# A fifth seven-product pair in each column pair of the down projection, in a new order of the pairs, with the MLP's squares on ScalarE

## The reference

```
proj = rmsnorm(x, norm1_g[l]) @ w_in[l]          # 2048 x 4352, split among the mixers A, B, C
x = x + concat(A, B, C) @ w_out[l]
h2 = rmsnorm(x, norm2_g[l])
x = x + square(relu(h2 @ w_up[l])) @ w_down[l]   # 2048 x 8192 and 8192 x 2048
```

## Time and profile before

| What | Value |
|---|---|
| Time, median of 3 runs | 2037.56 us (2037.42 to 2037.96) |
| The profiled execution: its own time | 2036.9 us |
| Its span | 2035.1 us |
| TensorE busy | 2028.2 us |
| VectorE busy | 1517.8 us |
| ScalarE busy | 1161.0 us |
| GpSimd busy | 228.0 us |

### The profile page before, as it was taken

One profiled execution on the slowest core, in us unless ns is written; L12 is line 12 of the kernel. 1 busy time (PEld: TensorE's weight loads), 2 busy tenths in 40 slices (PEclk: granted clock), 3 DMA queues, 4 the chain that ended last, 5 costly groups with the idle time before them and its releaser, 6 DMA issues.

```text
span 2035.1 us, 27169 instructions
## 1 busy us (share of the span) xinstructions
PE 2028.2 (100%) x10602; PEld 1702.0 (84%) x10602; DVE 1517.8 (75%) x1953; ACT 1161.0 (57%) x1540; POOL 228.0 (11%) x224
## 2 busy tenths in 40 slices
PE   9999999999999999999999999999999999999999
PEld 8887788888888888888888877888888888888887
DVE  7767566788779769868777775666887796797785
ACT  6557644466456457545545576445654564565463
POOL 6253100000000000002123531000000000000000
PEclk9999999999999999999999999999999999999999
DMA  9477866677668667766664778666776686677664
GB/s 304 131 230 190 219 199 181 185 217 230 187 196 246 197 197 211 224 189 202 199 177 142 219 196 229 187 183 188 228 216 189 196 244 193 202 214 219 189 205 137
DMA packets 182816, 411.36 MB, mean 202 GB/s; under 512 B 14122, under 2 KB 22800, under 8 KB 182688
## 3 DMA queue, kind: packets, MB, share of 16 engines
q1 hardware_dynamic: 173968, 379.52, 60.7%
q0 software_dynamic: 8544, 30.01, 8.1%
q10 hardware_dynamic: 176, 0.09, 0.0%
HBM read 377.95 MB, written 2.12 MB: 187 GB/s over the span
## 4 chain that ended last, share of the span: by engine, by line
PE 99%; DVE 1%; DMA 0%; issue 0%; SPq 0%; ACT 0%; ACTq 0%
PE psum L635 23%; PE psum L611 21%; PE psum L638 12%; PE psum L615 10%; PE psum L678 10%; PE psum L681 5%; PE psum L645 3%; PE psum L649 3%; PE psum L646 3%; PE psum L728 2%; PE psum L729 2%; PE psum L732 2%; PE psum L743 1%; PE psum L817 1%; PE psum L796 0%; PE psum L842 0%
## 5 line engine op out<-in xcount | busy, mean ns | idle before, releaser
L940 ACT CAST w_hi<-raw_ring 128x1024 fp32r<-128x1024 f32 (+1 forms) x720 | 743.7, 1041 | 710.1 <-PE psum L638 322.6
L1180 DVE TENSOR_TENSOR w_lo<-raw_ring,w_hi 128x1024 fp32r<-128x1024 f32 (+1 forms) x664 | 811.4, 1230 | 387.3 <-ACT w_hi L940 385.6
L635 PE MATMUL psum<-xt,w_hi 128*128 128x512 f32 x2048 | 513.3, 392 | 0.3 <-issue 0.3
L635 PEld LDWEIGHTS psum<-xt,w_hi 128*128 128x128 f32 x2048 | 368.8, 189 | 67.0 <-issue 0.7
L638 PEld LDWEIGHTS psum<-xt,w_lo 128*128 128x128 f32 x2048 | 279.4, 190 | 20.0
L638 PE MATMUL psum<-xt,w_lo 128*128 128x256 f32 x2048 | 285.6, 282 | 0.0
L611 PE MATMUL psum<-w_hi,xt 128*128 128x512 f32 (+1 forms) x1152 | 281.5, 386 | 0.1
L611 PEld LDWEIGHTS psum<-w_hi,xt 128*128 128x128 f32 x1152 | 202.4, 188 | 40.8 <-issue 2.9
L1737 POOL DMA_DIRECT2D lo_own<-raw_ring x28 | 24.3, 866 | 1361.2 <-ACT lo_own L956 1361.2
L678 PE MATMUL psum<-w_hi,ht_lo 128*128 128x512 f32 x448 | 174.4, 389 | 0.0
L678 PE MATMUL psum<-w_hi,ht_hi 128*128 128x512 f32 x448 | 174.4, 389 | 0.0
(11 more groups left out here) (212 smaller groups left out, 2462.1 us busy)
## 6 DMA issues: line engine op xcount, KB each, us to landing
raw_ring<-in_w_up_dram SPq DMA_DIRECT2D x256, 512.0 KB, 4.1
raw_ring<-in_w_down_dram SPq DMA_DIRECT2D x256, 512.0 KB, 4.6
raw_ring<-in_w_in_dram SPq DMA_DIRECT2D x128, 512.0 KB, 4.6
raw_ring<-in_w_out_dram SPq DMA_DIRECT2D x64, 512.0 KB, 4.9
w_lo<-raw_ring POOLq DMA_DIRECT2D x28, 512.0 KB, 6.6
lo_own<-raw_ring POOLq DMA_DIRECT2D x28, 512.0 KB, 6.8
raw_ring<-in_w_in_dram SPq DMA_DIRECT2D x16, 256.0 KB, 2.8
x<-in_x_dram SPq DMA_DIRECT2D x8, 256.0 KB, 7.6
```

The costliest lines, as they stand in the source:

```text
L635: pe.matmul(bank[:, f, :], w_hi[:, w, j, f * P:(f + 1) * P], both, start=kt == 0, stop=False, skip_group_check=True)
L940: act.copy(w_hi[:, u % AHEAD, :, 0:cols], raw_ring[:, u % RAWS, :, 0:cols]).then_inc(hi_ready, 1)
L1180: dve.tensor_tensor(w_lo[:, u % AHEAD, :, 0:cols], raw_ring[:, u % RAWS, :, 0:cols], w_hi[:, u % AHEAD, :, 0:cols].bitcast(F32), ALU.subtr ...
```

## The change

- The pairs of a column pair are taken in the order of `ORDER`, `kp` 0, 1, 3, 2, 5, 6, 4, 7, and the places 1, 2, 4, 5 and 7 of it use seven products (`SEVEN_AT`). So `kp = 6` (`EXTRA`) is new among them, and places 1 and 2, and 4 and 5, are neighbours.
- For the second of two neighbours, `t_hi` and `t_lo` are made two units later in the queues of ScalarE and VectorE (`follows_seven`), and its weight sums are begun behind the first one's `t_lo`.
- The token sums of `kp = 6` are made apart: VectorE at step 5 (`sums_of`), ScalarE's `extra_hi` at step 6, VectorE's `extra_lo` at step 7 of `d = 0`. TensorE waits for them (`extra_done`) before place 5. They lie over `head_in`, which is free by then.
- The other token sums move one step later.
- The last chunk: VectorE's two operations L1566 and L1568 become one (relu, times `row_scale`), and ScalarE squares the result twice, once into `ht_hi` and once in place. `row_scale` now holds the root, which GpSimd works out.
- The units with a low part by DMA are `m0` and `m12`, in place of `m0` and `m8`.
- Four transposes of x in the tail of layer 0 (`T_USE`, the x1 panels) come one step later.

```diff
@@ -76,15 +76,19 @@
 KPS = 8
 SEVEN = (1, 3, 5, 7)
 BLOCKS = {b: [kp % 4 for kp in SEVEN if kp // 4 == b] for b in range(2)}
-SEVENS = (LOOPS * 2 + 1) * len(SEVEN)
+EXTRA = 6
+ORDER = [(0, 1, 3, 2, 5, EXTRA, 4, 7)] * 2
+SEVEN_AT = [(1, 2, 4, 5, 7)] * 2
+TURN_SEVENS = sum(len(at) for at in SEVEN_AT)
+SEVENS = LOOPS * TURN_SEVENS + len(SEVEN_AT[0])
 BANK_MOVES = (2 * LOOPS + 1) * 4
...
 SUMMED_UNITS = list(range(55, 83, 2))
-SUMMED_PAIR = [LOOP0 + LOOP_UNITS * i + 16 * d + m for i in range(LOOPS) for d in range(2) for m in (0, 8)]
-SUMMED_PAIR += [DOWN3, DOWN3 + 8]
+SUMMED_PAIR = [LOOP0 + LOOP_UNITS * i + m for i in range(LOOPS) for m in (0, 12, 16, 28)]
+SUMMED_PAIR += [DOWN3, DOWN3 + 12]
...
 for _n in range(4):
-    T_USE[DOWN3 + 21 + 2 * _n] = ("x1", _n)
+    T_USE[DOWN3 + 22 + 2 * _n] = ("x1", _n)
...
+        with ExitStack() as extra:
+            extra_hi, extra_lo = [extra.enter_context(nc.sbuf_tensor(f"extra_{h}", [P, 4, P], F32R)) for h in ("hi", "lo")]
...
+        def follows_seven(pl, u):
+
+            return seven_at(pl, u) is not None and seven_at(pl, u - 2) is not None
...
-                kp, half = m // 2, m % 2
+                kp, half = ORDER[d][m // 2], m % 2
...
-                if kp in SEVEN:
+                if m // 2 in SEVEN_AT[d]:
...
-                i, first, last = SEVEN.index(kp), kp == SEVEN[0], kp == KPS - 1
+                first, last = kp == SEVEN[0], kp == KPS - 1
                 _, number = seven_at(pl, s)
                 if d == 0:
                     pe.wait_ge(s_done, pl.l * 2 * TURNS + 2 * pl.i + kp // 4 + 1)
+                if kp == EXTRA:
+                    pe.wait_ge(extra_done, pl.l * TURNS + pl.i + 1)
                 if first and d == 0:
                     pe.wait_ge(evicted[0], pl.evictions(18))
...
                 def s_tile(n):
-                    return [t[:, i, n, :] for t in (s_hi, s_lo)]
+                    if kp == EXTRA:
+                        return [t[:, n, :] for t in (extra_hi, extra_lo)]
+                    return [t[:, SEVEN.index(kp), n, :] for t in (s_hi, s_lo)]
...
                 act.wait_ge(unit_done, pl.unit(u + 1))
+                if follows_seven(pl, u - 2) and seven_at(pl, u - 2)[0] == 1:
+                    t_hi_of(seven_at(pl, u - 2)[1])
                 seven = seven_at(pl, u)
                 if seven is not None and seven[0] == 0:
                     act.wait_ge(t1_ready, seven[1] + 1)
                 act.copy(w_hi[:, u % AHEAD, :, 0:cols], raw_ring[:, u % RAWS, :, 0:cols]).then_inc(hi_ready, 1)
-                if seven is not None and seven[0] == 1:
-                    act.wait_ge(t_raw_ready, seven[1] + 1)
-                    if seven[1]:
-                        act.wait_ge(sevens_done, seven[1])
-                    act.copy(t_hi[:, :, :], t_raw[:, :, :]).then_inc(t_hi_ready, 1)
+                if seven is not None and seven[0] == 1 and not follows_seven(pl, u):
+                    t_hi_of(seven[1])
                 if is_summed(pl, u) and not has_own_lo(pl, u):
                     act.activation(w_lo[:, u % AHEAD, :, :], raw_ring[:, u % RAWS, :, :], ACT.Copy, scale=-1.0).then_inc(lo_negated, 1)
+
+            def t_hi_of(number):
+
+                act.wait_ge(t_raw_ready, number + 1)
+                if number:
+                    act.wait_ge(sevens_done, number)
+                act.copy(t_hi[:, :, :], t_raw[:, :, :]).then_inc(t_hi_ready, 1)
...
                     act.wait_ge(relu2, pl.at(H_CHUNKS, count + 1, 4))
-                    act.copy(ht[0][:, 4 * q:4 * q + 4, :].rearrange("p k n -> p (k n)"), mlp_t[q % 2][:, :]).then_inc(h_hi, 1)
-                made = sums_made(pl, s, part, c, k, 2)
+                    act.activation(ht[0][:, 4 * q:4 * q + 4, :].rearrange("p k n -> p (k n)"), mlp_t[q % 2][:, :], ACT.Square)
+                    act.activation(mlp_t[q % 2][:, :], mlp_t[q % 2][:, :], ACT.Square).then_inc(h_hi, 1)
+                made = sums_made(pl, s, part, c, k, 3)
                 if made is not None:
                     b, count = made
                     act.wait_ge(s_raw_ready, count + 1)
                     _, where, nb = s_places(b)
                     act.copy(s_hi[:, where, :, :], s_raw[:, 0:nb, :, :]).then_inc(s_hi_ready, 1)
+                if part == "pair" and c == 0 and k == 6:
+                    act.wait_ge(extra_raw, pl.l * TURNS + pl.i + 1)
+                    act.copy(extra_hi[:, :, :], s_raw[:, 0, :, :]).then_inc(extra_cast, 1)
...
+                if follows_seven(pl, u - 2) and seven_at(pl, u - 2)[0] == 1:
+                    t_lo_of(seven_at(pl, u - 2)[1])
+                after, seven = seven_at(pl, u + 1), seven_at(pl, u)
+                if after is not None and after[0] == 0 and seven is None:
                     first_sums(pl, u + 1)
-                seven = seven_at(pl, u)
                 if seven is not None and seven[0] == 0:
                     dve.wait_ge(t2_ready, seven[1] + 1)
                     dve.tensor_tensor(t_raw[:, 2, :], raw_ring[:, (u + 1) % RAWS, 0, :], t_raw[:, 1, :], ALU.subtract).then_inc(t_raw_ready, 1)
                 dve.wait_ge(hi_ready, pl.unit(u + 1))
                 dve.tensor_tensor(w_lo[:, u % AHEAD, :, 0:cols], raw_ring[:, u % RAWS, :, 0:cols],
                                   w_hi[:, u % AHEAD, :, 0:cols].bitcast(F32), ALU.subtract).then_inc(split_done, 1)
+                if seven is not None and seven[0] == 1:
+                    if pair_at(pl, u)[1:] == (1, 2 * SEVEN_AT[1][0] + 1):
+                        take_totals(pl, pair_at(pl, u)[0])
+                    if not follows_seven(pl, u):
+                        t_lo_of(seven[1])
+                    if after is not None:
+                        first_sums(pl, u + 1)
                 if after is not None and after[0] == 0:
                     dve.wait_ge(t1_ready, after[1] + 1)
                     dve.tensor_tensor(t_raw[:, 1, :], raw_ring[:, (u + 2) % RAWS, 1, :], raw_ring[:, (u + 1) % RAWS, 1, :],
                                       ALU.subtract).then_inc(t2_ready, 1)
-                if seven is not None and seven[0] == 1:
-                    if pair_at(pl, u)[1:] == (1, 2 * SEVEN[0] + 1):
-                        take_totals(pl, pair_at(pl, u)[0])
-                    dve.wait_ge(t_hi_ready, seven[1] + 1)
-                    dve.tensor_tensor(t_lo[:, :, :], t_raw[:, :, :], t_hi[:, :, :].bitcast(F32), ALU.subtract).then_inc(t_lo_ready, 1)
+
+            def t_lo_of(number):
+
+                dve.wait_ge(t_hi_ready, number + 1)
+                dve.tensor_tensor(t_lo[:, :, :], t_raw[:, :, :], t_hi[:, :, :].bitcast(F32), ALU.subtract).then_inc(t_lo_ready, 1)
...
-                fs = slice(own.start - 8 * b, own.stop - 8 * b, own.step)
+                sums_of(slice(own.start - 8 * b, own.stop - 8 * b, own.step), nb, s_raw_ready)
+
+            def sums_of(fs, nb, ready):
+
...
                 else:
-                    link(total)
-                    link(dve.tensor_scalar(tot, tot, 1.0 / D, EPS, ALU.mult, ALU.add))
-                    dve.reciprocal(rstd[:, 1, :], tot).then_inc(rstd_ready, 1)
+                    total.then_inc(row_total2, 1)
...
-                    link(dve.scalar_tensor_tensor(mlp_t[q % 2][:, :], mlp_t[q % 2][:, :], 0.0, mlp_t[q % 2][:, :], ALU.max, ALU.mult))
                     v = mlp_t[q % 2][:, :].rearrange("p (f q) -> p f q", f=4)
-                    dve.tensor_tensor(v, v, row_scale[:, :].unsqueeze(1).to_broadcast([P, 4, SEQ]), ALU.mult).then_inc(relu2, 1)
-                made = sums_made(pl, s, part, c, k, 1)
-                if made is not None:
-                    dve.wait_ge(relu2, late_count(pl, s))
-                    token_sums(made[0])
-                made = sums_made(pl, s, part, c, k, 3)
+                    dve.scalar_tensor_tensor(v, v, 0.0, row_scale[:, :].unsqueeze(1).to_broadcast([P, 4, SEQ]), ALU.max, ALU.mult).then_inc(relu2, 1)
+                made = sums_made(pl, s, part, c, k, 4)
...
+                made = sums_made(pl, s, part, c, k, 2)
+                if made is not None:
+                    token_sums(made[0])
+                if part == "pair" and c == 0 and k == 5:
+                    sums_of(slice(EXTRA % 4, EXTRA % 4 + 1), 1, extra_raw)
+                if part == "pair" and c == 0 and k == 7:
+                    dve.wait_ge(extra_cast, pl.l * TURNS + pl.i + 1)
+                    dve.tensor_tensor(extra_lo[:, :, :], s_raw[:, 0, :, :], extra_hi[:, :, :].bitcast(F32), ALU.subtract).then_inc(extra_done, 1)
...
+                    if u == SUMMED_PAIR[0]:
+                        pool.wait_ge(row_total2, pl.l + 1)
+                        rsqrt(rstd[:, 1, :], small[:, 4, 0:RT], RT, 1.0 / D).then_inc(rstd_ready, 1)
```

20 lines of the change are left out of this document (9 added, 11 removed).

## The result

The changed kernel takes 2140.82 us (median of 4 runs, 2139.66 to 2144.63), the kernel before 2037.49 us (4 runs, 2037.15 to 2037.96): a ratio of 1.051, 95% interval 1.0497 to 1.0524. It is 103 us slower. The forecast was 2123 us, in a range of 2085 to 2155. The profiled execution of after took 2139.92 us, its span 2138.1 us.

A forecast was written before the change was run, and what follows sets the result against it. TensorE was taken to bound the kernel, with VectorE nearly full in `d = 0`. Eight `d = 0` at +9.4 us, six `d = 1` at +1.9, less 1.3, gave 85.3, so 2123 us; range 2085 to 2155.

The forecast's parts named there:

- VectorE sets `d = 0`: In `d = 0`, VectorE, busy 38.90 of 41.2 us before, can't keep up; the half takes 50.6 us against 41.2.
- The ledger: VectorE's added work in `d = 0`: by amounts, the split of `m11` comes 4.9 us short, `extra_lo` some 7.3.
- Rival 2: Only amounts of work count: `d = 0` 6.2 us over, `d = 1` 0.8 under, 2081 us; chance 0.15.
- B in `d = 0`: Second seven-product pair: TensorE waits 1.9 us for `t_hi` and 2.9 for `t_lo`, ending 4.8 late.
- A: First of the five seven-product pairs in a column pair; in `d = 0` TensorE is done with it at 10.2 us.
- D's wait for `extra_lo`: Fourth seven-product pair of `d = 0`: TensorE waits 4.5 us, until 34.4, before its very first matmul.
- C: Third seven-product pair; in `d = 0` TensorE gets all of it in time and ends it at 29.9 us.
- E in `d = 0`: Fifth seven-product pair: ScalarE's negation waits for `m12`, the split of `m15` comes late, TensorE waits 1.2 us.
- `d = 1`: Second half of a column pair: waits of 2.7 us, so 42.8 us against 40.9.
- Costs nothing: GpSimd's root, ScalarE's second squares in the up stages, the DMA for `m12` and SyncE's reloads add no time.
- The clock: TensorE's granted clock: no row shows what waits of 3 to 4.5 us do; by rows alone the sum stays 85.
- rival 3: Lower clock for 21 matmuls behind the `extra_lo` wait: 4.8 us, 8 times, +38, so 2161 us; chance 0.14.

The follow-up runs named there:

- e11: Changed kernel with squares and negation later, second-half totals earlier, and 18 zero matmuls ahead of the fourth seven-product pair's wait: 2099.2 us.
- e4: Changed kernel without the token sums of `kp = 6`, using those of `kp = 5` in their place: 2110.6 us.
- e5: Changed kernel with VectorE's addition on the last chunk put back ahead of the second neighbour's weight sums: 2146.84 us.
- e7: Changed kernel with ScalarE's two squares one pair step later in `d = 0`, behind the cast of `m6`: 2135.03 us.
- e6: Changed kernel with ScalarE's negation for `m0` of `d = 1` three steps ahead in place of six: 2134.44 us.
- e2: Changed kernel with the fifth pair and new order in `d = 1` alone: 2047.77 us, ratio 1.0052 to the kernel before.
- e1: Changed kernel with the fifth pair taken back, the old order and DMA help at `m8`: 2035.88 us, ratio 0.9992 to the kernel before.
- e3: Changed kernel with the fifth pair and new order in `d = 0` alone: 2137.43 us.
- e12: The same kernel as e9, executed again: 2120.88 us, ratio 1.041 to the kernel before.
- e9: e7 with 18 zero matmuls put ahead of the fourth seven-product pair's wait in `d = 0`: 7273.11 us in its one execution.
- e8: e2 with VectorE's totals taken one unit sooner: 2040.5 us, ratio 1.0015 to the kernel before.

## Why the prediction came out as it did

The direction and the mechanism held; the time is 18 us above the forecast, 2 us inside the band of 2105 to 2143 that was called likeliest. Measured in the changed kernel, six turns take 576.7 us against 492.4 and the two `d = 0` at the ends of the layers 100.2 against 82.5: 102.0 us more, and 1.0 elsewhere. The forecast had 86.6 and -1.3.

- *VectorE sets `d = 0`.* Right. The ledger (4.9 us short by amounts, 7.3 with the totals) is what e11 is left with, and e4 gives 3.1 us for the token sums of `kp = 6`. Rival 2's price, 6.2 a `d = 0`, was too low even there (6.9 to 7.7 in e11).
- *B in `d = 0`.* Its lateness was put at 4.8 (1.9 for `t_hi`, 2.9 for `t_lo`) and is 5.2, but in other places. I gave A no wait. I did write that the chunk's addition moves behind three weight sums, and did not ask who waits for it: TensorE's A uses the banks that this addition empties. A waits 2.4 us, therefore `t_hi` is in time, and `t_lo` is waited for 2.4. e5 brought back the waits of the forecast and no time. That the missed wait left the sum nearly as it was is luck: it came where B was bound by VectorE anyway. And the trace before had shown it, small. There too A's first matmul follows this addition (424.10 + 1.22 = 425.32), 5.71 in instead of 5.44:

```profile
425.42 0.47 PE L645 MATMUL psum<-w_hi,ht_hi 128*128 128x512 f32 x1
```

  The squares on ScalarE were right: 0.97 and 0.94 from start to start, and VectorE idles 1.88 for the cast of `m6` where 1.9 was worked out; e7 took the 2 us out.
- *D's wait for `extra_lo`.* Put at 4.5, D starting 34.4 in; it starts 35.02 in. Two small terms: behind `t_lo` the next weight sum starts 1.88 us later (437.71 to 439.59; the same behind A's and C's), not 1.67, where the kernel waits for that very `t_lo`: 0.2 too little, three times. And four token sums of 128 take 1.05 (450.50 to 451.55), not 1.2. The Trainium skill, "VectorE: DVE Perf Modes", section "The TRN2 errata — SBUF-src ops pay a fixed extra latency per instruction", gives (N + 151) / 0.96 ns for a float32 addition of two tiles; by it 128 elements take an estimated 291 ns. The trace agrees, 0.28 to 0.29 us; I could have priced them there.
- *E in `d = 0`.* Put at 1.2, is 1.65: two restarts (0.47 for the cast, 0.65 for the split) in place of one. In the two `d = 0` that stand alone it is absent: no `d = 1` follows, nothing is negated, and they take 50.09. I had counted it eight times, it comes six times. e6 confirms mechanism and size.
- *`d = 1`.* Put at 42.8 and is 43.6. The bank's wait is 0.35 of idle time, and with the restart behind it the first pair ends 0.69 late (0.7 forecast), the totals push the split as worked out, and B ends 2.95 late, for 2.7 forecast (11.72 and 17.91 in for A and B, where 10.20 and 14.96 would be in time). D then waits for a split of its own and loses another 0.5, where I had all in time from C on. That VectorE's step behind each `t_lo` is 0.2 longer than I counted fits this, but was not tried alone. e2 shows that `d = 1` costs 2.0 us with an undisturbed `d = 0` too.
- *Costs nothing.* Root, up stages, squares there: right (e1). From first matmul to first matmul an up stage behind a turn takes 89.36 us in the kernel before, in e1 and in the changed kernel. The 1.3 us of the later transposes are gained in e1, where the way from the end of layer 0's last `d = 0` to the next pair stage is 456.15 us against 457.52. In the changed kernel a DMA comes late once for 1.6 us (the last of the waits above), and they are not to be seen.
- *The clock*, left out of the sum and priced at 38 us in rival 3: right in kind, far too dear. The lower level comes ten times in the changed kernel, 40.9 us in all. In two of the eight `d = 0` it falls on D, behind a wait of 4.45 us, and that half takes 53.98 instead of 51.74. In the other six it falls on the end of B and the plain pair behind it (440.63 to 443.19, rows above), which together end 1.6 us later (27.2 in, 25.6 in the two), and D's wait for VectorE is shorter by as much, 2.9: free. Free too are the last two of the ten, in A of the same two `d = 0`: B's wait for `t_lo` shrinks by them. I had priced all 21 matmuls; some 11 are slow (rows of 0.63 us), 2.2 us. The Trainium skill, "TensorE: Matmul & The Clock Gate", section "HAM oscillation — how this bites in real kernels", prices such stretches at half of their time, for each. For the two on D that comes out, 2.2 us for the 4.8 that lie on it; for the other eight it doesn't, since TensorE has a later wait that absorbs them.

The two windows of D in the changed kernel, first turn and second, the latter with a mean granted clock of 0.66:

```profile
455.21:460.06 4.85, 4.85 (x22) 4.03 (x23) 4.34 (x5) 1.30 (x2) 0.00 (x0) 1.00 0.80 230
639.91:647.03 7.12, 7.12 (x21) 5.65 (x22) 5.48 (x6) 1.30 (x2) 0.00 (x0) 0.66 0.75 242
```

So of the 17.7 us between the forecast sum (85.3) and what was measured (103.0), `d = 0` has 10.1 (85.3 for 75.2), of which the clock is 4.5, `d = 1` has 5.3 (16.7 for 11.4), and the rest of the program 2.3 (1.0 for -1.3). The mis-sized terms are `d = 0` and `d = 1`; no step failed in kind but that A has a wait, and that E's wait was also counted where no `d = 1` follows.

The best kernel of the study is e1, the change without its fifth pair, and it can't be told from the kernel before.

## What to carry to other kernels

Fewer matmuls are worth nothing where the engine that prepares them is nearly full: VectorE had 38.9 of 41.2 us in `d = 0`, and each new pair brings it 4.2 us to save TensorE 0.7. When an operation moves back in a queue, list who waits for each of its results, the buffer that it empties too. And when an edit removes a wait but the time stays, look at the clock right behind the next wait before giving up the theory: here that took back 1.6 of 2.0 us in five `d = 0` and more in the other three, and filling the idle time gave it back.

## What was not expected of the hardware

- The clock falls behind short waits. In the first turn it falls behind waits of 2.24 and 2.37 us with 9.1 us of matmuls between them (from 440.63 on they start 0.425 us apart). In the second turn the first of these is enough; A's first matmul and its seventh, 1.6 us later:

```profile
612.77 0.47 PE L653 MATMUL psum<-w_hi,ht_hi 128*128 128x512 f32 x1 [2.23 <-issue]
...
614.38 0.63 PE L653 MATMUL psum<-w_hi,ht_hi 128*128 128x512 f32 x1
```

  So the same wait, at the same place of the same program, brings the lower level at once in two of the eight and not in six. The kernel before, whose longest such wait is 1.3 us, has it nowhere between its first stage and its last.
- Which wait the fall lands behind changes when waits are moved, and with it the price: e3, e5, e6 and e7 each removed or moved a wait as expected and had 10 to 16 stretches at the lower level. So a single edit's time was off by up to 9 us from the sum of its waits (e3).
- Matmuls of zeros kept the level up: D's window in e12 at 1.00 in all eight, in e7 at 0.73 in the one shown.
- One execution with matmuls 0.84 us apart throughout (e9), 3.7 times the usual 0.227, and a granted clock of 1.00 in its records; and one of twice the time in e8 (4092.16), without a profile. In e9 VectorE and ScalarE ran at their usual durations.
